# Attention rows transposed inside the last projection chunk, and another order on VectorE in the branch merge

## The chip, the cores and the metric

The kernel runs on one core of one Trainium2 chip. The metric is the device time of the whole program in microseconds (us), lower is better. Three timed runs of the kernel before lie between 2477.99 and 2490.73 us, with a median of 2486.15 us.

## What is computed

Two transformer blocks of two layers each, over 256 rows of 1024 channels, all in float32. The change touches only the mixer of the first block, which runs once per layer. Cut to that part, the reference is:

```python
for l in range(2):
    ...
    h = rms_norm(x, mix_norm[l])
    (nq, ..., ngate, sq, sk, sv, wq, wk, wv, bgate) = jnp.split(h @ w_in[l], SPLIT_POINTS, axis=-1)
    y_nsa = nsa_attention(...)             # 512 channels
    y_sb = stick_breaking_attention(...)   # 256 channels
    y_swa = swa_sink_attention(...)        # 256 channels
    g = jax.nn.sigmoid(bgate).reshape(B, S, 3, 1024)
    merged = (g[:, :, 0] * (y_nsa @ w_up_nsa[l]) + g[:, :, 1] * (y_sb @ w_up_sb[l])
              + g[:, :, 2] * (y_swa @ w_up_swa[l]))
    x = x + merged @ w_out[l]
    ...
```

## The kernel before

The 256 rows are two tiles (t = 0, 1) of 128 partitions. Weights come in chunks of at most 128 x 2048 numbers (1 MB), loaded by SyncE into a ring of four slots, one transfer per chunk, in program order. A slot is loaded again when TensorE has finished the chunk in it (`chunks_done`).

Every product with a weight is made from three products of rounded parts. ScalarE writes the rounded weight (RH, two buffers, line 1366), VectorE the rest, weight minus RH (RL, line 1792). Both steps are called `split`. The activations have the same two parts, HTH (ScalarE, line 1351) and HTL (VectorE, line 1776), made by `ht_copy` from a transposed copy that TensorE left in PSUM. In `split_products`, TensorE runs RH x HTH (line 646) and RH x HTL (line 647) for the first items, waits for RL, runs RL x HTH (line 650) for those items, and then the remaining items with all three products each. A chunk has 24 products of 512 columns, or 48 of 256 columns.

The mixer's projection `h @ w_in` has 23 chunks, numbered 0 to 22 (loop over `j` on TensorE, over `i` on the other engines, N1 = 23). A projection chunk does the 8 items of row tile 0 first (its RL products come behind them), then the 8 items of row tile 1. The results of even chunks are copied out by ScalarE (line 1517), those of odd ones by VectorE (line 2066). The three attention branches run in pieces between the chunks. Their rows collect in Y; the last piece, the compressed branch, is made by TensorE behind chunk 21 (line 984, `oc_ready`) and added into Y by VectorE in turn 22 (line 2051, `src_ready`).

Behind chunk 22 come, on every engine in this order:

- TensorE transposes Y (`transpose_y`, line 699, 16 transposes into PSUM banks 2 to 5), and ScalarE and VectorE copy the result into HTH and HTL. Chunk 22 reads these same two buffers, so nothing of this can stand inside it.
- Chunks 23 and 24 (`w_up_nsa`, banks 4 to 7), 25 (`w_up_sb`, banks 0 to 3) and 26 (`w_up_swa`, banks 4 to 7). Chunk 26 waits until VectorE has read chunk 24's result (`rows_taken`).
- Meanwhile ScalarE turns the gate columns of the projection into sigmoids (lines 1531 and 1533).
- VectorE merges the branches: TMP = bank 4..7 x gate 0 (line 2081), Y = bank 0..3 x gate 1 (line 2086), TMP += Y (line 2087), and then, per row tile, Y = bank 4..7 x gate 2 (line 2093) and Y += TMP (line 2094, `merged_rows`). Each instruction waits for the one before it (`link`).
- TensorE transposes the merged Y in two halves (lines 711 and 715), ScalarE and VectorE copy it into HTH and HTL, and chunks 27 to 30 (`w_out`) follow. Chunk 27 starts when the first of four pieces of HTL is there.

The splits stand by hand between these steps. On VectorE the split of chunk 27 stands ahead of line 2086.

Of the kernel before, what the change touches and what calls it, by code (L numbers as in the profile page):

```python
# [10 lines left out]
ALU = mybir.AluOpType  # L11
# [3 lines left out]
P = 128  # L15
S = 256
T = S // P
D = 1024
K = D // P
# [6 lines left out]
W1 = [256] * 9 + [24] + [256] * 13  # L26
N1 = len(W1)
# [160 lines left out]
def build(nc, a, out, con, hot_rev, hot, vect, scratch):  # L188
    ctx = ExitStack()
    with ctx:  # L190
# [3 lines left out]
        def over(name, shape, at, dtype=F32R):  # L194

            return nc.alloc_sbuf_tensor_at(name, shape, dtype, offset=at).ap()
# [16 lines left out]
        at_tt = nc.sbuf_base  # L213
# [45 lines left out]
        RINGS = over("RINGS", [P, ESLOTS, SLOT], at_ring, F32)  # L259
        RL = over("RL", [P, ESLOTS, SLOT], at_ring)  # L260
        RH3 = over("RH3", [P, SLOT], at_kd)
        GH, GL = (over(n, [P, 22, S], at_proj + 4 * i * 22 * S) for i, n in enumerate(("GH", "GL")))
        MEMH, MEML = (over(n, [P, K, S], at_proj + 4 * (T * D_IN2 + i * K * S)) for i, n in enumerate(("MEMH", "MEML")))
        EHH, EHL = (over(n, [P, 4, S], at_proj + 4 * (T * D_IN2 + 2 * K * S + i * 4 * S)) for i, n in enumerate(("EHH", "EHL")))
# [33 lines left out]
        def spread(ap, at, n):  # L298

            return bass.AP(tensor=ap.tensor, offset=ap.offset, ap=[*ap.ap[:at], [0, n], *ap.ap[at:]])  # L300
# [150 lines left out]
        def tr1(l, k):  # L451
            return l * 5 + k
# [9 lines left out]
        def rows_src(block, l):  # L462
            return l if block == 0 else L + l
# [159 lines left out]
        def _(pe):  # L623
# [7 lines left out]
                pe.wait_ge(ring_full[slot], ring.full())  # L631
                return RINGS[:, slot, :]

            def split_products(width, early, items, ht=None, half=None):

                slot = ring.next()
                splits.n += 1  # L640

                pe.wait_ge(wh_ready, splits.v + splits.n)
                listed = items(splits.buffer(RH, RH3)[:, 0:width], RL[:, slot, 0:width])

                def rounded(dst, a_, b_, start, stop, left):
                    mm(dst, a_[0], b_[0], start=start, stop=False)  # L646
                    mm(dst, a_[0], b_[1], start=False, stop=False) if left else mm(dst, a_[1], b_[0], start=False, stop=False)  # L647

                def rest(dst, a_, b_, start, stop, left):
                    return mm(dst, a_[1], b_[0], start=False, stop=stop) if left else mm(dst, a_[0], b_[1], start=False, stop=stop)  # L650

                for i, item in enumerate(listed[:early]):
                    if ht is not None and i < K and i % 2 == 0:
                        ht_wait(ht, i // 2)
                    rounded(*item)

                pe.wait_ge(wl_ready, splits.v + splits.n)
                for item in listed[:early]:
                    last = rest(*item)
                if half is not None:  # L660
                    last.then_inc(half, 1)
                for item in listed[early:]:
                    rounded(*item)
                    last = rest(*item)
                last.then_inc(chunks_done, 1)
# [6 lines left out]
                             (rhs[0][:, k, :], rhs[1][:, k, :]), k == 0, k == K - 1, True) for c in range(2) for k in range(K)]  # L672
                split_products(SLOT, K, items, ht)

            def to_rows(width, bank_of, lhs, at=0, ht=None):

                def items(wh, wl):
                    wh, wl = (w.rearrange("p (k n) -> p k n", n=width) for w in (wh, wl))
                    return [(PS[:, bank_of(t), at * t:at * t + width], (lhs[0][:, k, t * P:(t + 1) * P], lhs[1][:, k, t * P:(t + 1) * P]),
                             (wh[:, k, :], wl[:, k, :]), k == 0, k == K - 1, False) for t in range(T) for k in range(K)]  # L680
                split_products(K * width, K if at else 2 * K, items, ht)

            def add_rows(bank, lhs, k0, first, end, tiles=T, half=None):

# [37 lines left out]
            def transpose_y(n, made, bank=0):  # L722

                pe.wait_ge(ht_l, n * 4 + 4)
                pe.wait_ge(src_ready, made + 1)
                transpose_rows(Y, n, bank)

            def ht_wait(n, bank=3):

                pe.wait_ge(ht_l, n * 4 + bank + 5)  # L730
# [36 lines left out]
            def rows_product(lhs, nchunk, bank, k0=0, ht=None, half=None):  # L767

                for j in range(nchunk):
                    if ht is not None:  # L770
                        ht_wait(ht, k0 // 2 + j)
                    add_rows(bank, lhs, k0 + 2 * j, j == 0, j == nchunk - 1, half=half if j == nchunk - 1 else None)
# [5 lines left out]
            for l in range(L):  # L778
# [82 lines left out]
                for j in range(N1):  # L861
                    if j >= 2:
                        col_taken(j - 2)
                    to_rows(W1[j], lambda t: j % 2, HT, at=256, ht=n if j == 0 else None)
                    if 8 <= j < 8 + NU:
                        if j == 8:
                            pe.wait_ge(tt_a, l * 4 + 3)
# [117 lines left out]
                                          VCB.rearrange("p h d -> p (h d)"), start=True, stop=True)  # L985
                        last.then_inc(oc_ready, 1)

                n = tr1(l, 2)
                transpose_y(n, rows_src(0, l), 2)
                ht_wait(n)  # L990
                col_taken(21)
                col_taken(22)
                rows_product(HT, 2, 4)
                rows_product(HT, 1, 0, k0=4)

                pe.wait_ge(rows_taken, l + 1)
                rows_product(HT, 1, 4, k0=6, half=up_half)
                n = tr1(l, 3)
                transpose_halves(Y, n, merged_rows, 2 * l + 1)
                rows_product(HT, 4, 4, ht=n, half=rows_half)  # L1000
# [322 lines left out]
        def _(act):  # L1323
# [21 lines left out]
            def ht_copy(n, dst, gains=None, tiles=K, bank=0):  # L1345

                for b in range(4):

                    act.wait_ge(tr_ready, n * 4 + b + 1)
                    if gains is None or 2 * b >= tiles:  # L1350
                        A(dst[0][:, 2 * b:2 * b + 2, :], PS[:, bank + b, :].rearrange("p (k n) -> p k n", k=2), ACT.Copy).then_inc(ht_h, 1)
                    else:
                        A(dst[0][:, 2 * b, :], PS[:, bank + b, 0:S], ACT.Copy, scale=LV[:, gains + 2 * b:gains + 2 * b + 1])
                        A(dst[0][:, 2 * b + 1, :], PS[:, bank + b, S:2 * S], ACT.Copy, scale=LV[:, gains + 2 * b + 1:gains + 2 * b + 2]).then_inc(ht_h, 1)
# [61 lines left out]
            for l in range(L):  # L1416
# [32 lines left out]
                for i in range(N1):  # L1449
# [53 lines left out]
                    if i == 21:  # L1503
                        act.wait_ge(pct_ready, l + 1)
                        A(PTF[:, 0, 0:512], PS[:, 7, :], ACT.Copy).then_inc(pct_taken, 1)
                    if 9 <= i < 9 + NU:
                        exps(i - 9)
                    if i in (14, 15, 16):
# [16 lines left out]
                        ahead.skip(2)  # L1525
                        split(SLOT, 6)

                ht_copy(tr1(l, 2), HT, bank=2)
                act.wait_ge(col_d, cols_d + N1 // 2)
                act.wait_ge(col_a, cols_a + N1 // 2 + 1)  # L1530
                A(PROJ[:, :, BG:BG + D], PROJ[:, :, BG:BG + D], ACT.Sigmoid).then_inc(branch_gates, 1)
# [223 lines left out]
        def _(dve):  # L1755
# [11 lines left out]
                ring.next()  # L1767
                dve.wait_ge(chunks_done, ring.done())

            def ht_copy(n, dst, gains=None, tiles=K, bank=0):  # L1770

                for b in range(4):

                    dve.wait_ge(ht_h, n * 4 + b + 1)
                    if gains is None or 2 * b >= tiles:
                        TTn(dst[1][:, 2 * b:2 * b + 2, :], PS[:, bank + b, :].rearrange("p (k n) -> p k n", k=2), dst[0][:, 2 * b:2 * b + 2, :].bitcast(F32),  # L1776
                            ALU.subtract).then_inc(ht_l, 1)
                    else:
                        for k in (2 * b, 2 * b + 1):
                            last = V.scalar_tensor_tensor(dst[1][:, k, :], PS[:, bank + b, (k % 2) * S:(k % 2 + 1) * S], LV[:, gains + k:gains + k + 1],  # L1780
                                                          dst[0][:, k, :].bitcast(F32), ALU.mult, ALU.subtract)
                        last.then_inc(ht_l, 1)


            ahead, splits = Ring(), Splits()
# [78 lines left out]
            for l in range(L):  # L1864
# [83 lines left out]
                for i in range(N1):  # L1948
# [95 lines left out]
                        dve.wait_ge(osb_ready, l + 1)  # L2044
                        V.tensor_copy(Y[:, :, 512:768], PS[:, 6, :].rearrange("p (t n) -> p t n", t=2))
                    if i == 22:
                        dve.wait_ge(oc_ready, l + 1)
                        for t in range(T):
                            for r in range(2):
                                y = Y[:, t, 0:512].rearrange("p (g r x) -> p r g x", g=2, r=2)[:, r]  # L2050
                                last = TTn(y, y, PS[:, 4 + t, r * 256:(r + 1) * 256].rearrange("p (g x) -> p g x", g=2), ALU.add)
                        last.then_inc(src_ready, 1)
                    if 9 <= i < 9 + NU:
                        softmax(i - 9)
                    if 11 <= i < 11 + NU:
# [8 lines left out]
                    if i % 2:  # L2064
                        w = W1[i]
                        TTn(PROJ[:, :, OFF1[i]:OFF1[i] + w], PS[:, 1, :].rearrange("p (t n) -> p t n", t=2)[:, :, 0:w],
                            spread(SMALL[:, 4:6], 2, w), ALU.mult).then_inc(col_d, 1)
                    if i <= 10 or i >= 16:
                        split(K * W1[i + 2] if i + 2 < N1 else SLOT)
                    elif i in (12, 13):  # L2070
                        ahead.skip(2)
                        split()

                ht_copy(tr1(l, 2), HT, bank=2)
                split()
                ring.n += 1
                chunk()
# [3 lines left out]
                TTn(TMP, high, bg[0], ALU.mult).then_inc(rows_taken, 1)  # L2081
                split()
                chunk()
                split()
                dve.wait_ge(branch_gates, 2 * l + 2)
                link(TTn(Y, low, bg[1], ALU.mult))
                link(TTn(TMPF, TMPF, YF, ALU.add))
                for t in range(T):
# [3 lines left out]
                        chunk()  # L2092
                    link(TTn(Y[:, t, :], high[:, t, :], bg[2][:, t, :], ALU.mult))
                    TTn(Y[:, t, :], TMP[:, t, :], Y[:, t, :], ALU.add).then_inc(merged_rows, 1)
                ht_copy(tr1(l, 3), HT)
                split()
                for j in range(3):
                    split()
# [430 lines left out]
```

## Time and profile before

| | before |
|---|---|
| median of three timed runs | 2486.15 us |
| the profiled execution, its time | 2483.38 us |
| its span, first to last instruction | 2481.6 us |
| TensorE products busy | 2362.2 us, 95% of the span |
| VectorE busy | 1541.1 us, 62% |
| ScalarE busy | 1185.4 us, 48% |
| GpSimd busy | 71.7 us, 3% |
| mean granted clock of TensorE | 0.961 of 2.4 GHz |
| chain of work that ended last | TensorE 87%, VectorE 7%, ScalarE 3% |

The chain of work that ended last is the sequence of instructions, each released by the one before, that leads to the end of the program. Work outside it is hidden. The trace has a timeline (instructions of one engine in order of time, neighbours of one line merged), a view of waits, and a view that gives busy times and the granted clock of any stretch.

### The profile page before, as it was taken

Reading aid. Unit: us, or ns where it says so; the run is one execution under the profiler, and the core shown is the slowest. Engines: PE = TensorE matmul, PEld = TensorE weight load, DVE = VectorE, ACT = ScalarE, POOL = GpSimd, SP = SyncE. Lnnn points to the kernel's source line nnn. Section 1 sums busy time; section 2 is a strip of 40 time slices with the busy share of each in tenths; the row PEclk is TensorE's granted clock in tenths of the full one; section 3 lists DMA queues with packets and bytes.
Section 4 is the critical chain, followed back from the end, with each engine's and each line's share of the span. In section 5 each row is a group of like instructions: output and inputs, shape, how many; then the busy total and the mean of one; then the engine's idle time right before and its main releaser. Section 6 shows DMA issues by size and latency. Waiting matters only on the chain.

```text
span 2481.6 us, 34563 instructions
## 1 busy us (share of the span) xinstructions
PE 2362.2 (95%) x15120; PEld 2126.2 (86%) x15120; DVE 1541.1 (62%) x1421; ACT 1185.4 (48%) x1154; POOL 71.7 (3%) x84
## 2 busy tenths in 40 slices
PE   8999999799999998998999999799998999799998
PEld 8998889699899888887997999688887999688886
DVE  4655556566466446456664556478887556478887
ACT  3333543443343344434433445267775444267775
POOL 1000100000000001000000000000001000000000
PEclk9999899899999998999999999799999999799999
DMA  6554334355555543434555455389996455379995
GB/s 216 187 187 153 121 105 153 119 170 187 187 170 187 187 155 103 155 103 145 194 187 179 144 183 171 120 288 348 347 367 229 152 173 178 121 282 347 354 361 198
DMA packets 309612, 490.92 MB, mean 198 GB/s; under 512 B 15348, under 2 KB 204964, under 8 KB 309456
## 3 DMA queue, kind: packets, MB, share of 16 engines
q1 hardware_dynamic: 305696, 475.35, 56.3%
q0 software_dynamic: 2912, 10.13, 1.3%
q10 hardware_dynamic: 848, 3.15, 0.3%
q8 instruction: 123, 2.02, 0.3%
q14 instruction: 33, 0.27, 0.0%
HBM read 487.52 MB, written 1.07 MB: 197 GB/s over the span
## 4 chain that ended last, share of the span: by engine, by line
PE 87%; DVE 7%; ACT 3%; issue 1%; POOL 1%; DMA 0%; DVEq 0%; POOLq 0%; ACTq 0%
PE PS L646 26%; PE PS L647 26%; PE PS L650 25%; ACT RH L1366 2%; DVE RL L1792 2%; PE PS L1258 1%; PE PS L857 1%; PE PS L822 1%; PE PS L1191 1%; PE PS L1264 1%; PE PS L807 1%; DVE HTL L1776 1%; ACT PR L1432 0%; POOL SMALL L597 0%; DVE HTL L1780 0%
## 5 line engine op out<-in xcount | busy, mean ns | idle before, releaser
L1792 DVE TENSOR_TENSOR RL<-RINGS,RH 128x2048 fp32r<-128x2048 f32 x450 | 1018.3, 2265 | 638.0 <-ACT RH L1366 635.1
L1366 ACT ACTIVATE RH<-RINGS 128x2048 fp32r<-128x2048 f32 x450 | 852.0, 1894 | 834.4 <-PE PS L650 833.9
L646 PE MATMUL PS<-RH,HTH 128*128 128x256 f32 (+3 forms) x1888 | 627.9, 343 | 25.0 <-DVE HTL L1776 16.5
L647 PE MATMUL PS<-RH,HTL 128*128 128x256 f32 (+3 forms) x1888 | 614.1, 335 | 0.0
L650 PE MATMUL PS<-RL,HTH 128*128 128x256 f32 (+3 forms) x1888 | 450.5, 330 | 0.0
L646 PEld LDWEIGHTS PS<-RH,HTH 128*128 128x128 f32 x1888 | 373.7, 198 | 66.6 <-DVE HTL L1776 17.7
L646 PE MATMUL PS<-HTH,RH 128*128 128x256 f32 x1536 | 408.2, 284 | 9.2 <-ACT RH L1366 5.0
L647 PE MATMUL PS<-HTL,RH 128*128 128x256 f32 x1536 | 405.0, 282 | 0.0
L647 PEld LDWEIGHTS PS<-RH,HTL 128*128 128x128 f32 x1888 | 374.7, 198 | 32.6 <-issue 0.2
L650 PEld LDWEIGHTS PS<-RL,HTH 128*128 128x128 f32 x1888 | 332.4, 195 | 34.0
L650 PE MATMUL PS<-HTH,RL 128*128 128x256 f32 x1536 | 324.4, 283 | 0.0
L646 PEld LDWEIGHTS PS<-HTH,RH 128*128 128x128 f32 x1536 | 292.0, 190 | 12.9 <-issue 10.8
L647 PEld LDWEIGHTS PS<-HTL,RH 128*128 128x128 f32 x1536 | 291.6, 190 | 0.1
L650 PEld LDWEIGHTS PS<-HTH,RL 128*128 128x128 f32 x1536 | 244.6, 190 | 0.0
L646 PE MATMUL PS<-RH,GH 128*128 128x512 f32 x352 | 139.8, 397 | 0.0
L647 PE MATMUL PS<-RH,GL 128*128 128x512 f32 x352 | 137.9, 392 | 0.0
L647 PE MATMUL PS<-RH,EHL 128*128 128x512 f32 x256 | 100.7, 393 | 0.0
L646 PE MATMUL PS<-RH,EHH 128*128 128x512 f32 x256 | 100.5, 392 | 0.0
L650 PE MATMUL PS<-RL,GH 128*128 128x512 f32 x352 | 90.2, 391 | 0.0
L646 PEld LDWEIGHTS PS<-RH,GH 128*128 128x128 f32 x352 | 66.1, 188 | 16.2
L650 PEld LDWEIGHTS PS<-RL,GH 128*128 128x128 f32 x352 | 66.1, 188 | 14.9
L647 PEld LDWEIGHTS PS<-RH,GL 128*128 128x128 f32 x352 | 66.1, 188 | 14.4
(397 smaller groups left out, 2193.0 us busy)
## 6 DMA issues: line engine op xcount, KB each, us to landing
RINGS<-w_in SPq DMA_DIRECT2D x64, 1024.0 KB, 5.2
RINGS<-w_gate SPq DMA_DIRECT2D x64, 1024.0 KB, 5.7
RINGS<-w_up SPq DMA_DIRECT2D x64, 1024.0 KB, 5.6
RINGS<-w_down SPq DMA_DIRECT2D x64, 1024.0 KB, 5.4
RINGS<-ffn_w_gate SPq DMA_DIRECT2D x44, 1024.0 KB, 5.2
RINGS<-ffn_w_up SPq DMA_DIRECT2D x44, 1024.0 KB, 5.2
RINGS<-ffn_w_down SPq DMA_DIRECT2D x44, 1024.0 KB, 4.9
RINGS<-w_out SPq DMA_DIRECT2D x16, 1024.0 KB, 4.9
```

What stands on the lines that cost most here:

```text
L646: mm(dst, a_[0], b_[0], start=start, stop=False)
L647: mm(dst, a_[0], b_[1], start=False, stop=False) if left else mm(dst, a_[1], b_[0], start=False, stop=False)
L650: return mm(dst, a_[1], b_[0], start=False, stop=stop) if left else mm(dst, a_[0], b_[1], start=False, stop=stop)
L807: last = nc.tensor.transpose(PS[:, 4 + i // 4, (i % 4) * P:(i % 4 + 1) * P], PRF[:, u % 2, i * P:(i + 1) * P], IDENT)
L822: last = mm(PS[:, 6, s_ * HD:(s_ + 1) * HD], PTF[:, u % 2, i * P:(i + 1) * P], PROJ[:, b, vc:vc + HD], start=(b == 0), stop=(b == t))
L857: last = mm(PS[0:64, 7, kv * 256:(kv + 1) * 256], BT[:, kv, i * 8 + r, :], w[:, r, :], start=(i + r == 0), stop=(i == 1 and r == 7))
L1191: last = nc.tensor.transpose(PS[:, 2 + at // 512, at % 512:at % 512 + P], EHID[:, t, k * P:(k + 1) * P], IDENT)
L1258: last = mm(PS[:, 6 + i, k * P:(k + 1) * P], X[:, t, (4 * i + k) * P:(4 * i + k + 1) * P], SEAT[:, g, t, :], start=(t == 0), stop=(t == T ...
L1264: return mm(PS[:, 6 * t + h, :], SEATT[:, g, t, :], YSEAT[g][part][:, h, :], start=(g + part == 0), stop=(g + part == NG_))
L1366: A(splits.buffer(RH, RH3)[:, 0:width], RINGS[:, slot, 0:width], ACT.Copy).then_inc(wh_ready, 1)
L1776: TTn(dst[1][:, 2 * b:2 * b + 2, :], PS[:, bank + b, :].rearrange("p (k n) -> p k n", k=2), dst[0][:, 2 * b:2 * b + 2, :].bitcast(F32), AL ...
L1792: TTn(RL[:, slot, 0:width], RINGS[:, slot, 0:width], splits.buffer(RH, RH3)[:, 0:width].bitcast(F32), ALU.subtract).then_inc(wl_ready, 1)
```

## The change

Three edits, in each of the two layers:

1. Y is transposed in the middle of chunk 22, between its first eight items and the rest (`between`), and the copies go into YT, which lies over the first 16 of the 20 tiles of TT. Chunks 23 to 26 read YT.
2. For that, VectorE adds the compressed branch into Y in turn 21, ahead of the split of chunk 23. `ht_copy` moves into turn 22, on both engines ahead of the wait for chunk 22. TensorE's waits for the results of chunks 21 and 22 move behind chunks 23 and 24.
3. VectorE's split of chunk 27 moves from ahead of line 2086 to behind the first piece of the merged rows' HTL (`behind`).

```diff
+        YT = [over(n, [P, K, S], at_tt + 4 * i * K * S) for i, n in enumerate(("YTH", "YTL"))]
...
-            def split_products(width, early, items, ht=None, half=None):
+            def split_products(width, early, items, ht=None, half=None, between=None):
...
                 if half is not None:
                     last.then_inc(half, 1)
+                if between is not None:
+                    between()
                 for item in listed[early:]:
...
-                    to_rows(W1[j], lambda t: j % 2, HT, at=256, ht=n if j == 0 else None)
+                    to_rows(W1[j], lambda t: j % 2, HT, at=256, ht=n if j == 0 else None,
+                            between=(lambda: transpose_y(tr1(l, 2), rows_src(0, l), 2)) if j == N1 - 1 else None)
...
-                n = tr1(l, 2)
-                transpose_y(n, rows_src(0, l), 2)
-                ht_wait(n)
+                ht_wait(tr1(l, 2))
+                rows_product(YT, 2, 4)
                 col_taken(21)
                 col_taken(22)
-                rows_product(HT, 2, 4)
-                rows_product(HT, 1, 0, k0=4)
+                rows_product(YT, 1, 0, k0=4)
...
-                rows_product(HT, 1, 4, k0=6, half=up_half)
+                rows_product(YT, 1, 4, k0=6, half=up_half)
...
# ScalarE
+                    if i == 22:
+                        ht_copy(tr1(l, 2), YT, bank=2)
...
-                ht_copy(tr1(l, 2), HT, bank=2)
...
# VectorE
-            def ht_copy(n, dst, gains=None, tiles=K, bank=0):
+            def ht_copy(n, dst, gains=None, tiles=K, bank=0, behind=None):
...
+                    if b == 0 and behind is not None:
+                        behind()
...
                     if i == 22:
-                        dve.wait_ge(oc_ready, l + 1)
-                        for t in range(T):
-                            for r in range(2):
-                                y = ...
-                                last = TTn(y, y, ..., ALU.add)
-                        last.then_inc(src_ready, 1)
+                        ht_copy(tr1(l, 2), YT, bank=2)
...
+                    if i == 21:
+                        (the five removed lines, behind the result of chunk 21 is copied out)
...
-                ht_copy(tr1(l, 2), HT, bank=2)
                 split()
...
                 TTn(TMP, high, bg[0], ALU.mult).then_inc(rows_taken, 1)
                 split()
                 chunk()
-                split()
                 dve.wait_ge(branch_gates, 2 * l + 2)
...
-                ht_copy(tr1(l, 3), HT)
+                ht_copy(tr1(l, 3), HT, behind=split)
```

## Rows read from the trace of the kernel before

**Rows 1.** Page, first line.
```profile
span 2481.6 us, 34563 instructions
```
**Rows 2.** Waits of PE, 425 to 480 us: total us, times, longest.
```profile
PE PS L711 <- DVE Y L2094: 6.4, 1, 6.4
PE PS L646 <- DVE HTL L1776: 5.8, 1, 5.8
```
**Rows 3.** Timeline of PE, layer 0: start, us, instruction, [idle before, releaser].
```profile
426.65 1.89 PE L984 MATMUL PS<-VCB,PT 128*128 128x256 f32 x8
...
431.23 0.28 PE L646 MATMUL PS<-RH,HTH 128*128 128x256 f32 x1
...
434.12 1.91 PE L699 MATMUL PS<-CON,Y 128*128 128x128 f32 x16
441.80 0.80 PE L646 MATMUL PS<-RH,HTH 128*128 128x512 f32 x1 [5.77 <-DVE HTL L1776]
...
449.59 0.40 PE L646 MATMUL PS<-RH,HTH 128*128 128x512 f32 x1
...
455.15 0.40 PE L646 MATMUL PS<-RH,HTH 128*128 128x512 f32 x1
...
458.87 1.99 PE L650 MATMUL PS<-RL,HTH 128*128 128x512 f32 x8
...
472.74 1.94 PE L711 MATMUL PS<-CON,Y 128*128 128x128 f32 x8 [6.35 <-DVE Y L2094]
...
477.14 0.80 PE L646 MATMUL PS<-RH,HTH 128*128 128x512 f32 x1
```
**Rows 4.** Chain that ended last: start of chunk 28, layer 0.
```profile
484.57 0.23 PE PS L646
```
**Rows 5.** Timeline of DVE, layer 0.
```profile
431.09 1.40 DVE L2051 TENSOR_TENSOR Y<-Y,PS 128x256 f32<-128x256 f32 x4
...
463.25 2.29 DVE L1792 TENSOR_TENSOR RL<-RINGS,RH 128x2048 fp32r<-128x2048 f32 x1 [3.42 <-ACT RH L1366]
465.46 2.28 DVE L2086 TENSOR_TENSOR Y<-PS,PROJ 128x2048 f32<-128x2048 f32 x1
...
473.76 1.23 DVE L2094 TENSOR_TENSOR Y<-TMP,Y 128x1024 f32<-128x1024 f32 x1
476.40 2.48 DVE L1776 TENSOR_TENSOR HTL<-PS,HTH 128x512 fp32r<-128x512 f32 x4 [1.41 <-ACT HTH L1351]
```
**Rows 6.** Timeline of ACT, layer 0.
```profile
436.85 2.05 ACT L1351 ACTIVATE HTH<-PS 128x512 fp32r<-128x512 f32 x4
...
440.21 1.91 ACT L1531 ACTIVATE PROJ<-PROJ 128x2048 f32<-128x2048 f32 x1
...
451.68 3.61 ACT L1533 ACTIVATE PROJ<-PROJ 128x4096 f32<-128x4096 f32 x1
...
461.24 1.92 ACT L1366 ACTIVATE RH<-RINGS 128x2048 fp32r<-128x2048 f32 x1 [3.91 <-PE PS L650]
```
**Rows 7.** Page, part 6: ring transfers of w_out, us from issue to landing.
```profile
RINGS<-w_out SPq DMA_DIRECT2D x16, 1024.0 KB, 4.9
```
**Rows 8.** Timelines of PE, then DVE, layer 1.
```profile
1107.62 0.79 PE L646 MATMUL PS<-RH,HTH 128*128 128x512 f32 x1 [5.77 <-DVE HTL L1776]
...
1124.61 1.99 PE L650 MATMUL PS<-RL,HTH 128*128 128x512 f32 x8
...
1130.93 2.28 DVE L2086 TENSOR_TENSOR Y<-PS,PROJ 128x2048 f32<-128x2048 f32 x1
```
**Rows 9.** Stretches elsewhere: busy PE, PEld, DVE, ACT, POOL; then PEclk, DMA share, GB/s.
```profile
273.50:276.00 2.50, 0.04 (x1) 0.00 (x0) 1.94 (x3) 2.49 (x2) 0.53 (x1) 0.97 0.51 137
276.00:279.40 3.40, 3.36 (x17) 3.39 (x17) 1.29 (x3) 0.88 (x3) 0.00 (x0) 0.52 0.61 212
1476.30:1479.10 2.80, 0.04 (x1) 0.03 (x1) 1.11 (x2) 2.40 (x2) 0.00 (x0) 1.00 0.53 140
1479.10:1482.00 2.90, 2.90 (x13) 2.38 (x14) 1.58 (x1) 0.00 (x0) 0.00 (x0) 1.00 0.57 232
```

More of the change, by code:

```diff
@@ L673, in to_columns, with to_rows @@
                 split_products(SLOT, K, items, ht)
-            def to_rows(width, bank_of, lhs, at=0, ht=None):
+            def to_rows(width, bank_of, lhs, at=0, ht=None, between=None):
                 def items(wh, wl):
@@ L680, in items @@
                              (wh[:, k, :], wl[:, k, :]), k == 0, k == K - 1, False) for t in range(T) for k in range(K)]
-                split_products(K * width, K if at else 2 * K, items, ht)
+                split_products(K * width, K if at else 2 * K, items, ht, between=between)
             def add_rows(bank, lhs, k0, first, end, tiles=T, half=None):
@@ L2046, in _ @@
                     if i == 22:
-                        dve.wait_ge(oc_ready, l + 1)
-                        for t in range(T):
-                            for r in range(2):
-                                y = Y[:, t, 0:512].rearrange("p (g r x) -> p r g x", g=2, r=2)[:, r]
-                                last = TTn(y, y, PS[:, 4 + t, r * 256:(r + 1) * 256].rearrange("p (g x) -> p g x", g=2), ALU.add)
-                        last.then_inc(src_ready, 1)
+                        ht_copy(tr1(l, 2), YT, bank=2)
                     if 9 <= i < 9 + NU:
@@ L2067, in _ @@
                             spread(SMALL[:, 4:6], 2, w), ALU.mult).then_inc(col_d, 1)
+                    if i == 21:
+                        dve.wait_ge(oc_ready, l + 1)
+                        for t in range(T):
+                            for r in range(2):
+                                y = Y[:, t, 0:512].rearrange("p (g r x) -> p r g x", g=2, r=2)[:, r]
+                                last = TTn(y, y, PS[:, 4 + t, r * 256:(r + 1) * 256].rearrange("p (g x) -> p g x", g=2), ALU.add)
+                        last.then_inc(src_ready, 1)
                     if i <= 10 or i >= 16:
```

## The prediction

> **What bounds the kernel now.** I read the page's busy shares and its chain of work first: TensorE is busy 95% of the span and carries 87% of the chain, so time is won only where TensorE stands still or runs at the lower clock. The view of TensorE's waits then gives the places. The two that the change can touch come once per layer, 5.8 us for HTL and 6.4 us for the merged rows [rows 2]. The timeline shows what stands around them.
>
> First pause: the 16 transposes start at 434.12 and take 1.91 us, so they end at 436.03, and chunk 23 starts at 441.80 after 5.77 us of idling [rows 3]. In between ScalarE and VectorE finish chunk 24's split and make HTH and HTL. The first product behind the pause takes 0.80 us where those at the start of chunks 24 and 25 take 0.40 [rows 3]: the granted clock fell to 1.2 GHz while TensorE idled. Chunk 23 therefore lasts from 441.80 to 449.59, 7.79 us, against 5.56 us for chunk 24 (449.59 to 455.15) [rows 3].
>
> Second pause: chunk 25 ends at 458.87 + 1.99 = 460.86 [rows 3], but line 2086, the first that needs it, starts at 465.46 [rows 5]. Ahead of it in VectorE's queue stands the split of chunk 27, which waits for the RH that ScalarE writes from 461.24 [rows 6] and then takes 2.29 us [rows 5]. From the start of line 2086 to the end of the merge (473.76 + 1.23 = 474.99) there are 9.53 us of linked work [rows 5], and chunk 27 starts 2.15 us behind that, at 477.14 [rows 3].
>
> **The change part by part.** Sums are made against the profiled execution, span 2481.6 us [rows 1], time 2483.4 us; its time is 2.8 us under the median of the runs and inside their scatter.
>
> *Transposes in chunk 22, results in memory of their own.* Nothing is added: 16 transposes, 4 copies on ScalarE and 4 subtractions on VectorE move ahead. TensorE keeps their 1.8 us or so. The question is whether anything arrives too late in the new place.
> - The transposes need Y complete. The compressed branch's products end at 426.65 + 1.89 = 428.54 [rows 3]. VectorE has copied out chunk 21 by then, adds from 428.6 for 1.40 us [rows 5] and is done at 430.0. TensorE reaches the middle of chunk 22 at 431.23 [rows 3]. Slack 1.2 us. Queued behind the new wait on VectorE is the split of chunk 23, which moves from about 431.1 to 432.3 at its end; chunk 23 wants it at about 440.
> - Transposes from 431.25 to 433.05, then the second half of chunk 22 until about 436.2 (chunk 22 ends at about 434.3 now, while the transposes behind it are starting; 1.8 for the transposes and 0.1 from the bound below come on top). ScalarE copies as the pieces come, 2.05 us [rows 6], done about 434.1; VectorE, free at 432.3, is done about 435.0 (2.48 us for four [rows 5]). Slack 1.2 us before chunk 23 wants them at 436.2.
> - ScalarE passes its copies ahead of the copying out of chunk 22 and the split of chunk 24. That split now ends at about 438.8 instead of 436.95, chunk 24 wants it at 441.8. The sigmoid of gate 0 still ends near 442.1, as before (440.21 + 1.91 [rows 6]), since what was ahead of it is only reordered. The RH of chunk 25 then comes at 444.0, the second sigmoid (3.61 us [rows 6]) at 447.6, the RH of chunk 26 at 449.5.
> - VectorE: TMP from 447.5 to 449.8, RL of chunk 26 until 452.1. Chunk 26 starts at 452.9 and needs both, RL not before 454.7.
> - No DMA is issued or moved by the edit itself, and neither SyncE nor GpSimd has a step inside it. SyncE's loads follow `chunks_done` and so come earlier with it: the first w_out chunk is released at the end of chunk 23, 441.8, lands 4.9 us later [rows 7], and ScalarE wants it at 452.9.
>
> So the pause of 5.77 us goes, and with it the fall of the clock: 7.79 - 5.56 = 2.23 us. Together 8.0 us. What the trace of before does not show is 16 transposes in the middle of a chunk. Lower bound 0 (they cost the same in any place); upper bound 0.4 us, by which the first product behind the transposes and the pause is longer than one in full flow (0.80 against 0.40 [rows 3]). Most of those 0.4 is the clock, so I take 0.1. Per layer 7.9 us.
>
> *The split of chunk 27 behind the first piece.* Line 2086 can start about 0.2 us behind chunk 25's end instead of 465.46 - 460.86 = 4.6 us: gain 4.4 us in layer 0. Layer 1: 1130.93 - (1124.61 + 1.99) = 4.33 [rows 8], gain 4.1. What is late next is the linked merge of 9.5 us itself, which starts at 453.1 and ends at 462.5; TensorE ends chunk 26 at 458.45 and idles for some 1.6 us before the first half of the rows, where it idled 6.35 us. The moved split costs 2.29 us behind the first subtraction. Chunk 27 starts at 464.6 and wants that RL after its 16 first products, at 468.3 or later; it is there at 467.0. The three other HTL pieces end at about 469, the next is wanted at 470.2 at the earliest. Both covers hold, the thinner by 1.3 us; without them each late us costs one.
>
> *The clock in the second pause.* Before, it cost 484.57 - 477.14 = 7.43 us [rows 3, 4] instead of 5.56 for chunk 27, and some 0.3 us in the last transposes. After, TensorE idles 1.6 us, transposes, waits about 1.5 us, transposes, waits 1 us: 6.1 us with only 1.8 to 2 us of work. Nearest rows: a pause of 2.5 us was followed by 1.2 GHz [rows 9], one of 2.8 us was not [rows 9]. Broken up over 6 us it is nearer to the first, so I take the clock as fallen again: gain 0, bounds 0 and 1.87 + 0.3 = 2.2 us per layer.
>
> Sum: layer 0, 7.9 + 4.4 = 12.3; layer 1, the same pause of 5.77 us and the same slow first product (0.79 us) [rows 8], 7.9 + 4.1 = 12.0. Together 24.3 us. From 2483.4 that is 2459.1 us, from the median 2461.8. I say 2460.
>
> **The rivals.**
> 1. *The clock stays up in the second pause.* Another 2 x 2.2 = 4.4 us: 2454.7 to 2457.4 us, say 2456. For it: the single pauses are shorter than 2.8 us [rows 9]. Against it: there are three in a row. The Trainium skill ("TensorE: Matmul & The Clock Gate", Part 1 on the HAM clock gate) says that an idle array is throttled and that what follows starts at the lower rate; by that rule the clock falls here and the sum stays 2460, without it 2456. The trace agrees at the pause of 2.5 us and does not at that of 2.8 us.
> 2. *A thin cover breaks.* If VectorE's copies for YT come 2 us later than I lay out, or RL of chunk 27 comes behind the sixteenth product, TensorE waits there. Losing the whole merge gain gives back 8.5 us: 2468.5 us. For it: slacks of only 1.2 to 1.3 us at three places. Against it: all durations there are rows of the same instructions.
> 3. *The change doesn't do what it says.* TensorE still stands still behind chunk 22, because YT or the operands of chunk 23 come only after it (copying out of chunk 22 first, say). Then only the merge gain is left, 8.5 us: 2477 us, within 0.5%. The order of the queues speaks against it, since `ht_copy` stands ahead of the wait for chunk 22 on both engines.
> 4. *Slower.* The transposes put 16 short products of 128 columns into a dense stream, and the clock could fall there and stay down. Place: from 431 us on, chunks 23 and later. Price: at half the clock a chunk takes up to twice its 5.56 us, so 5.6 us more. It decides from four chunks per layer on: 2 x 4 x 5.56 = 44.5 us against 24.3 gained, 2503.6 us; with three it would be 33.4 against 24.3, or 2492.5, still within 0.5% of no change. Against it: the 16 transposes take 1.91 us right behind chunk 22 now, and the 8 at the second pause 1.94 [rows 3], so the former run at full clock.
>
> **How the numbers follow.** Forecast 2460 us with 0.55; rival 1 0.27; rival 2 0.11; rival 3 0.04; rival 4 0.03. The range goes from 2449 (rival 1, less the 6 to 8 us by which single runs of before lie off their median) to 2471 (rival 2 with a little of the same). 0.5%, 12.4 us, is about what a measurement of this kernel can tell from no change. Faster by more than that: the forecast, rivals 1 and 2 except for a small part: 0.92. Within it: rival 3 and what is left: 0.05. Slower: 0.03.
>
> **What would show it.** In the profile after: the transposes of line 699 of both layers inside chunk 22, two groups of 256-column products around them; no idle time ahead of the first 512-column product and none of that kind over 0.45 us in chunk 23; line 2086 within 0.3 us of chunk 25's end; chunk 27 starting some 28.4 us behind chunk 22's end (now 477.14 - 434.3 = 42.8); chunk 27 lasting 7.4 us (forecast) or 5.6 us (rival 1). The prediction is wrong if TensorE waits for `src_ready` in chunk 22, for HTL at chunk 23, or for RL of chunk 27, or if the clock falls at a place where it was full before.

## The result

| | before | after |
|---|---|---|
| median of four timed runs each | 2486.28 us | 2454.22 us |
| ratio, 95% interval | | 0.988, 0.9845 to 0.9916 |
| the profiled execution, its time | 2483.38 us | 2456.64 us |
| its span | 2481.6 us | 2454.8 us |
| mean granted clock of TensorE | 0.961 | 0.967 |

The change makes the kernel 1.2% faster, 32.1 us between these two medians. The forecast was 2460 us with a range of 2449 to 2471; the median lies inside it, but the case that came was the first rival, the clock that stays up, at "2454.7 to 2457.4". Taken over all runs of both kernels in this study, the changed one has a mean of 2455.8 us (14 runs, standard deviation 3.9) and the one before 2484.7 us (23 runs, 3.4): 28.9 us, with a standard error of about 1.3.

### The profile page after: what moved, and what is told of

It is laid out like the page before. It is cut to its first block, busy times and chain, and to the rows that moved or that the text cites. A ratio compares the mean times of both kernels' runs of the same rounds, so it can differ in the third digit from the quotient of the medians.

```text
span 2454.8 us, 34563 instructions
## 1 busy us (share of the span) xinstructions
PE 2352.6 (96%) x15120; PEld 2119.5 (86%) x15120; DVE 1541.3 (63%) x1421; ACT 1185.7 (48%) x1154; POOL 71.7 (3%) x84
## 4 chain that ended last, share of the span: by engine, by line
PE 88%; DVE 6%; ACT 3%; issue 1%; POOL 1%; DMA 0%; POOLq 0%; DVEq 0%; ACTq 0%
PE PS L647 26%; PE PS L648 26%; PE PS L651 26%; ACT RH L1368 1%; PE PS L1260 1%; DVE RL L1797 1%; PE PS L860 1%; PE PS L825 1%; PE PS L1193 1%; PE PS L1266 1%; PE PS L810 1%; ACT PR L1434 0%; DVE HTL L1783 0%; POOL SMALL L598 0%; POOL SMALL L584 0%
## 5 line engine op out<-in xcount | busy, mean ns | idle before, releaser
L647 PE MATMUL PS<-RH,HTH 128*128 128x256 f32 (+3 forms) x1824 | 599.2, 339 | 15.1 <-DVE HTL L1779 6.8
L648 PE MATMUL PS<-RH,HTL 128*128 128x256 f32 (+3 forms) x1824 | 586.4, 332 | 0.0
L651 PE MATMUL PS<-RL,HTH 128*128 128x256 f32 (+3 forms) x1824 | 433.3, 328 | 0.0
L647 PEld LDWEIGHTS PS<-RH,HTH 128*128 128x128 f32 x1824 | 360.3, 198 | 51.8 <-issue 13.3
L648 PEld LDWEIGHTS PS<-RH,HTL 128*128 128x128 f32 x1824 | 361.3, 198 | 29.4 <-issue 0.2
L651 PEld LDWEIGHTS PS<-RL,HTH 128*128 128x128 f32 x1824 | 320.3, 196 | 31.4
```

## The profile after

The page of the changed kernel: the span, and what TensorE is busy.

```profile
span 2454.8 us, 34563 instructions
...
PE 2352.6 (96%) x15120; PEld 2119.5 (86%) x15120; DVE 1541.3 (63%) x1421; ACT 1185.7 (48%) x1154; POOL 71.7 (3%) x84
```

The instructions are as many as before, and VectorE and ScalarE are busy as long as before. TensorE is busy 9.6 us less with the same 15120 products. In the two stretches that the change touches it is 11.4 us less (90.25 us before, 78.81 after), in products that ran at 1.2 GHz before; elsewhere it is 1.8 us more. (In the changed kernel the lines 646, 647, 650 are 647, 648, 651; 699 is 702; 711 and 715 are 714 and 718; 2086 and 2094 are 2091 and 2099.)

TensorE's waits between 426 and 480 us, total us, times, longest. They answer to [rows 2], where the two largest were 6.4 and 5.8:

```profile
PE PS L714 <- DVE Y L2099: 1.8, 1, 1.8
PE PS L718 <- DVE Y L2099: 1.2, 1, 1.2
PE PS L647 <- DVE HTL L1779: 0.8, 1, 0.8
```

The 5.8 us ahead of chunk 23 are gone. The timeline of TensorE, layer 0, answers to [rows 3]: start, us, instruction, idle before.

```profile
431.54 1.91 PE L702 MATMUL PS<-CON,Y 128*128 128x128 f32 x16
433.20 0.36 PE L647 MATMUL PS<-RH,HTH 128*128 128x256 f32 x1
...
436.14 0.39 PE L647 MATMUL PS<-RH,YTH 128*128 128x512 f32 x1
...
460.29 1.06 PE L714 MATMUL PS<-CON,Y 128*128 128x128 f32 x8 [1.76 <-DVE Y L2099]
462.59 1.09 PE L718 MATMUL PS<-CON,Y 128*128 128x128 f32 x8 [1.24 <-DVE Y L2099]
464.44 0.50 PE L647 MATMUL PS<-RH,HTH 128*128 128x512 f32 x1 [0.76 <-DVE HTL L1779]
...
470.12 0.39 PE L647 MATMUL PS<-RH,HTH 128*128 128x512 f32 x1
```

The transposes stand inside chunk 22 with no wait ahead of them, and chunk 23 (the first product of 512 columns) follows chunk 22 without a gap and at full clock, 0.39 us instead of 0.80. Behind chunk 26 one long pause of 6.35 us (and a short one of 0.36 between the halves) has become three of 1.76, 1.24 and 0.76 us. Each half of the transposes takes 1.06 and 1.09 us; before, the first took 1.94 [rows 3]. VectorE in the same time, which answers to [rows 5]:

```profile
428.88 1.41 DVE L2073 TENSOR_TENSOR Y<-Y,PS 128x256 f32<-128x256 f32 x4 [1.03 <-PE PS L988]
430.21 2.28 DVE L1797 TENSOR_TENSOR RL<-RINGS,RH 128x2048 fp32r<-128x2048 f32 x1
432.80 2.48 DVE L1779 TENSOR_TENSOR YTL<-PS,YTH 128x512 fp32r<-128x512 f32 x4 [0.31 <-ACT YTH L1353]
...
453.01 2.29 DVE L2091 TENSOR_TENSOR Y<-PS,PROJ 128x2048 f32<-128x2048 f32 x1 [1.06 <-PE PS L651]
...
463.70 0.69 DVE L1779 TENSOR_TENSOR HTL<-PS,HTH 128x512 fp32r<-128x512 f32 x1 [1.16 <-ACT HTH L1353]
464.31 2.28 DVE L1797 TENSOR_TENSOR RL<-RINGS,RH 128x2048 fp32r<-128x2048 f32 x1
466.50 1.88 DVE L1779 TENSOR_TENSOR HTL<-PS,HTH 128x512 fp32r<-128x512 f32 x3
```

The sum into Y ends at 430.3, 1.2 us before TensorE wants it. YTL is whole at 435.3, 0.9 us before chunk 23. The merge (line 2091) waits for TensorE now and no longer for a split. RL of chunk 27 is there at 466.6; its RL products start at 468.27.

The granted clock behind chunk 26 (busy PE, PEld, DVE, ACT, POOL; then PEclk, DMA share, GB/s):

```profile
458.50:460.30 1.80, 0.04 (x2) 0.04 (x1) 1.77 (x3) 1.68 (x1) 0.00 (x0) 1.00 0.34 50
460.30:464.40 4.10, 2.15 (x16) 1.67 (x16) 2.91 (x4) 1.57 (x4) 0.00 (x0) 1.00 0.59 240
464.40:470.10 5.70, 5.66 (x24) 4.62 (x25) 5.70 (x5) 0.73 (x2) 0.00 (x0) 1.00 0.00 0
```

It is 1.00 throughout, although TensorE idles for almost 4 of the 6 us up to chunk 27.

**Where the time went.** In every trace I measured one stretch on TensorE's timeline: from the start of the compressed branch's products behind chunk 21 to the start of chunk 28. In us:

| | layer 0 | layer 1 | gain, both |
|---|---|---|---|
| before | 57.75 | 57.45 | |
| after, three profiles | 43.14 to 43.17 | 43.16 to 43.18 | 28.9 |

The stretch of before ends where the first product of chunk 28 starts, which is a line that neither the rows nor the prediction show:

```profile
484.40 0.40 PE L646 MATMUL PS<-RH,HTH 128*128 128x512 f32 x1
```

So the stretches alone are enough for the difference of the means; that the two agree to 0.1 us is luck, given the standard error. In layer 0 the 14.6 us are: 5.97 up to chunk 23, 2.20 from there to the end of chunk 26, 4.84 from there to chunk 27, 1.58 in chunk 27. In layer 1 they are 5.95, 2.12, 4.56 and 1.66.

Single runs of one kernel differ by several us, and the traces show part of the reason. The clock also falls at some fifteen other places, and which of them differs from run to run. Added up in steps of 1 us over the whole span, the time at the lower clock is 194.7 us in the profile of before and 160.5, 150.8 and 170.8 us in the three of the changed kernel, whose spans are 2454.8, 2449.2 and 2457.7 us. It is not the whole reason: of the timed runs of the changed kernel two have the same mean granted clock, 0.968, and last 2454.3 and 2460.9 us.

## The experiments

All of them are judged by the stretch, which repeats within 0.04 us as long as the clock does the same, and by the whole time where several rounds were run.

**The changed kernel beside the others (e0_after, e10_after).** No edit.

> The changed kernel again, on the chip of the three beside it, so that they are compared with it and not only with the kernel before. If the gain is what the two traces show for the two stretches (14.6 and 14.3 us), 28.9 us under the kernel before. If part of the gain lay elsewhere or was scatter, 25 us or less.

> The changed kernel once more, five rounds, beside the kernel with w_up_nsa last. 31 us under the kernel before, as in the rounds before.

Medians 2454.28 us (four runs, ratio 0.9878, 0.9862 to 0.9895) and 2457.35 us (six runs, 0.9891, 0.9872 to 0.991), 31.6 and 27.7 us under the kernel before on the same chip, where 28.9 and 31 were expected. Both are within the scatter. In both profiles, in both layers, the clock stays at full speed through the stretch.

**The transposes alone (e1_transposes).**

```diff
                 split()
                 chunk()
+                split()
                 dve.wait_ge(branch_gates, 2 * l + 2)
...
-                ht_copy(tr1(l, 3), HT, behind=split)
+                ht_copy(tr1(l, 3), HT)
```

> The change without its third edit: transposes inside chunk 22, but VectorE's split of chunk 27 stays ahead of the merge. Theory (the first pause and its low clock are worth 7.9 us per layer, and the second stays as it was, 6.4 us of idling and a fallen clock behind it): 15.8 us under the kernel before, chunk 27 lasting 7.4 us in both layers. Rival (the low clock at the second pause came from the first one, so the transposes alone keep it up): chunk 27 lasts 5.6 us, 19.6 us under the kernel before or more.

Median 2473.44 us, ratio 0.9956 (0.9939 to 0.9973). The stretches are 48.66 and 48.47 us, 18.1 us under before together. The medians differ by only 12.4 us, and the interval ends at 15.2: the whole time shows less than the stretches of the one profile do. That profile, 2466.01 us, is the fastest of the four runs, and the others have the same mean granted clock (0.961 to 0.963 against 0.962), so the clock isn't what makes them longer. Where the rest went stays open. The second pause and what follows, layer 0:

```profile
467.55 1.94 PE L714 MATMUL PS<-CON,Y 128*128 128x128 f32 x8 [6.32 <-DVE Y L2100]
469.85 1.97 PE L718 MATMUL PS<-CON,Y 128*128 128x128 f32 x8 [0.36 <-DVE Y L2100]
```
```profile
471.90:478.30 6.40, 6.35 (x24) 5.16 (x25) 3.98 (x4) 0.74 (x2) 0.00 (x0) 0.87 0.00 0
```

The pause and the slow transposes are as before, as the theory had it, so the low clock there comes from that pause and not from the first one: the rival falls. But chunk 27 lasts 6.4 us and not 7.4; the clock came back earlier in it (0.87 over the chunk). That, about 0.9 us per layer, is most of why the gain in the stretch is 18.1 and not 15.8.

**The moved split alone (e2_split).** The third edit put into the kernel before.

```diff
... (`ht_copy` gets `behind` as in the change)
                 chunk()
-                split()
                 dve.wait_ge(branch_gates, 2 * l + 2)
...
-                ht_copy(tr1(l, 3), HT)
+                ht_copy(tr1(l, 3), HT, behind=split)
```

> The kernel before with the third edit alone: the split of chunk 27 behind the first piece of HTL. Theory (the length of one uninterrupted pause decides on the clock, and this edit shortens the second one from 6.35 us to below 2): merge gain 4.3 us plus 2.1 us of clock per layer, 12.8 us under the kernel before, chunk 27 lasting 5.6 us; e1 and e2 add up to the whole change. Rival (the clock stays up there only since nothing fell at the first pause): chunk 27 lasts 7.4 us, 8.6 us under the kernel before.

Median 2471.81 us, ratio 0.9951 (0.9934 to 0.9968); stretches 52.08 and 52.11 us, 11.0 us under before. Transposes, then chunk 27, layer 0:

```profile
470.10:474.50 4.40, 3.03 (x16) 2.40 (x16) 2.95 (x4) 1.58 (x4) 0.00 (x0) 0.75 0.57 231
474.50:480.60 6.10, 6.09 (x24) 4.99 (x25) 6.10 (x5) 0.69 (x2) 0.00 (x0) 0.90 0.00 0
```

Neither case came. The pauses are those of the changed kernel (1.79 and 1.24 us), yet the clock fell between the two halves of the transposes, in both layers, and rose again early in chunk 27, which lasts 6.2 us. In the stretches the parts add up: 18.1 + 11.0 = 29.1 us against 28.9 for both. That is partly chance: each part alone still has a fall behind chunk 26 that the whole has not, and each of these falls costs less than the one of before. The medians, 12.4 and 14.1 us under before, add up to 26.5 us against 31.6 for the whole on the same chip, within their intervals.

**A longer pause (e3_pause_long, e4_pause_mid).** The first step of the merge done twice, for both row tiles or for one.

```diff
+                link(TTn(Y, low, bg[1], ALU.mult))
                 link(TTn(Y, low, bg[1], ALU.mult))
```

> The changed kernel with the first step of the merge (line 2091, 2.3 us) done twice, so that TensorE's first pause behind chunk 26 grows from 1.8 to 4.1 us. Theory (one uninterrupted pause decides on the clock): the clock falls, the stretch up to chunk 28 grows by 2.3 + 2.0 us in each layer. Rival (the clock stays up because the transposes break the stretch, however long its parts): 2.3 us per layer and chunk 27 at 5.6 us.

> The same with only row tile 0 of that step done twice (1.2 us), first pause 3.0 us. The traces so far have a pause of 2.5 us with a fall and one of 2.8 us without, so the theory leaves it open here and the rival says no fall: 1.3 us per layer without a fall, 3.3 us with one.

e3: first pause 4.09 us. Layer 0 transposes, layer 1 pause and transposes:

```profile
465.60:470.00 4.40, 3.91 (x16) 3.11 (x16) 2.96 (x4) 1.37 (x3) 0.00 (x0) 0.50 0.06 23
...
1117.50:1121.60 4.10, 0.04 (x1) 0.00 (x0) 4.03 (x4) 1.91 (x1) 0.00 (x0) 1.00 0.70 244
1121.60:1126.00 4.40, 3.03 (x16) 2.42 (x16) 2.95 (x4) 1.34 (x3) 0.00 (x0) 0.64 0.03 11
```

The stretch grows by 4.5 and 4.2 us, 2.3 of it work and 2.1 and 1.9 the clock: the theory's numbers. But the fall comes inside the pause in layer 0 and behind it in layer 1. e4: first pause 3.02 us, the clock full during it and at 0.77 over the transposes, chunk 27 at 6.24 us; the stretch grows by 2.07 us in both layers, 1.3 of it work and 0.8 the clock. So there is a third case beside the two that I had priced, a short fall that costs 0.8 us.

**The covers (e5_add_late, e6_col_waits).** e5 puts VectorE's sum into Y behind the split of chunk 23, as before the change; e6 puts TensorE's waits for chunks 21 and 22 back ahead of chunk 23.

```diff
# e6
+                col_taken(21)
+                col_taken(22)
                 rows_product(YT, 2, 4)
-                col_taken(21)
-                col_taken(22)
```

> The changed kernel with VectorE's sum for the compressed branch behind the split of chunk 23 in turn 21, where it stood in time before. It then ends at about 432.8 instead of 430.2, and TensorE reaches the middle of chunk 22 at 431.5. Theory (slack 1.2 us, each us beyond it costs one): TensorE waits 1.1 to 1.4 us inside chunk 22 in each layer, 2.5 us in all. Rival (the wait is taken up by idle time elsewhere): no change.

> The changed kernel with TensorE's waits for the results of chunks 21 and 22 ahead of chunk 23, where they stood before. ScalarE copies chunk 22 out until about 0.9 us behind its end. Theory: TensorE waits 0.9 to 1.1 us ahead of chunk 23 in each layer, 2 us in all, and the clock stays. Rival: nothing, since the weight loads of chunk 23 run ahead anyway.

e5, then e6, TensorE's timeline:

```profile
431.85 1.94 PE L702 MATMUL PS<-CON,Y 128*128 128x128 f32 x16 [1.25 <-DVE Y L2078]
```
```profile
440.21 0.47 PE L647 MATMUL PS<-RH,YTH 128*128 128x512 f32 x1 [1.13 <-ACT PROJ L1521]
...
466.75 1.97 PE L718 MATMUL PS<-CON,Y 128*128 128x128 f32 x8 [1.24 <-DVE Y L2099]
```

The waits are there and of the size expected, 1.25 and 1.13 us; chunk 23 comes 1.45 and 1.29 us later. The stretch, however, grows by 3.0 and 3.7 us in e5 and by 2.2 us in both layers in e6. Behind chunk 26 both have the first two pauses of the changed kernel, 1.76 and 1.24 us, and the clock falls all the same: in e6 at the start of the second half of the transposes, in e5 in chunk 27 in layer 0 (7.23 us) and in the wait between the two halves in layer 1 (chunk 27 then takes 7.65 us). The expectation of e6, that the clock stays, was wrong. This was the surprise, and the next experiment is about it.

**The same stretch, later (e8_shift).** Nothing of the stretch's waits is touched; TensorE's products behind chunk 21 are issued twice.

```diff
-                        for t in range(T):
-                            for r in range(2):
+                        for t, r in [(t, r) for _ in range(2) for t in range(T) for r in range(2)]:
```

> The changed kernel with TensorE's products of the compressed branch behind chunk 21 done twice (the same values), so that everything behind them comes 1.6 us later and the pauses behind chunk 26 keep their lengths (1.8, 1.2 and 0.8 us). Theory (whether the clock falls there hangs on where the stretch lies in time, not on its pauses alone): with this shift the clock can fall as in the two kernels shifted by 1.3 and 1.4 us, behind the first transposes or in chunk 27, and the stretch grows by 1.6 plus 0.8 to 2.2 us. Rival (in those two it was the wait of TensorE inside or ahead of chunk 23 that brought the fall): the clock stays up and the stretch grows by 1.6 us alone.

The halves of the transposes on TensorE's timeline, layer 0, and the granted clock around them:

```profile
464.53 1.06 PE L714 MATMUL PS<-CON,Y 128*128 128x128 f32 x8 [1.77 <-DVE Y L2098]
466.84 1.97 PE L718 MATMUL PS<-CON,Y 128*128 128x128 f32 x8 [1.24 <-DVE Y L2098]
```
```profile
464.50:466.80 2.30, 1.06 (x8) 0.85 (x8) 2.25 (x2) 0.27 (x1) 0.00 (x0) 0.88 0.93 379
466.80:468.90 2.10, 1.97 (x8) 1.57 (x8) 0.71 (x2) 1.34 (x3) 0.00 (x0) 0.50 0.14 55
```

Chunk 23 comes 1.74 us later with no wait ahead of it, the pauses behind chunk 26 are 1.77 and 1.24 us as in the changed kernel, and the clock falls in the wait ahead of the second half of the transposes in both layers. The stretch is 47.0 us: 1.7 us of work and 2.1 us of clock over the changed kernel. So no wait of TensorE is needed for such a fall, and the rival falls. It is one profile of one kernel; what supports it is the place of the pauses.

That place can be read from the traces. Within each of the fourteen, the moments at which the granted clock changes lie on one even grid, within 4 ns, through the whole program. Take the place of the first pause behind chunk 26 as the time since the last grid moment:

| kernels with pauses of 1.8 and 1.2 us | the first pause begins behind a grid moment by | clock |
|---|---|---|
| changed kernel, three profiles | 1.4, 1.4; 1.7, 1.7; 1.4, 1.4 us (layers 0, 1) | stays full |
| e2, e6, e8 | 2.9, 2.9; 2.9, 2.9; 3.3, 3.4 us | falls |
| e5 | 0.2, 3.1 us | falls in chunk 27; falls between the halves |

All six stretches of the changed kernel lie together on this grid, and all eight that lost the clock with the same pauses lie elsewhere on it.

**The up projections in another order (e7_nsa_last, e11_nsa_last, e9_nsa_shift).** A version meant to beat the changed kernel: with the two chunks of w_up_nsa last, the sums of the other two branches run under them. Its core:

```diff
# TensorE
-                rows_product(YT, 2, 4)
+                rows_product(YT, 1, 4, k0=4)
                 col_taken(21)
                 col_taken(22)
-                rows_product(YT, 1, 0, k0=4)
+                rows_product(YT, 1, 0, k0=6)
...
-                rows_product(YT, 1, 4, k0=6, half=up_half)
+                rows_product(YT, 2, 4, half=up_half)
# VectorE
-                split()
-                ring.n += 1
                 chunk()
                 dve.wait_ge(branch_gates, 2 * l + 1)
-                TTn(TMP, high, bg[0], ALU.mult).then_inc(rows_taken, 1)
+                TTn(TMP, high, bg[1], ALU.mult).then_inc(rows_taken, 1)
                 split()
                 chunk()
                 dve.wait_ge(branch_gates, 2 * l + 2)
-                link(TTn(Y, low, bg[1], ALU.mult))
+                link(TTn(Y, low, bg[2], ALU.mult))
+                split()
                 link(TTn(TMPF, TMPF, YF, ALU.add))
+                ring.n += 1
```

e9 is this kernel with e8's edit. ScalarE makes the sigmoid of gate 1 first.

> A possible better version: the changed kernel with the order of the up projections turned, w_up_sb (banks 4 to 7), w_up_swa (banks 0 to 3), then the two chunks of w_up_nsa. What is left of the merge behind chunk 26 is one product and one sum per row tile, the rest runs under chunks 24 and 25. Theory (the linked merge is what TensorE waits for in the changed kernel, 9.5 us from the end of chunk 25): merged rows at about 2.6 us behind chunk 26 instead of 4.2, so 1.6 us per layer, 3 us under the changed kernel. Rival (something else comes late there, such as VectorE's splits or the sigmoids, which now have to be there for gate 1 first): no gain, or a wait ahead of chunk 25 of w_up_nsa.

> The kernel with w_up_nsa last, with the same products done twice. Its pauses behind chunk 26 are 1.6 and 0.8 us, with no pause ahead of the first transposes. Theory (shorter pauses keep the clock wherever they lie): chunk 27 at 5.7 us, the stretch 1.6 us longer than in that kernel without the shift. Rival (place in time decides here too): a fall behind the transposes, 0.8 us or more on top.

> The kernel with w_up_nsa last, five rounds. Theory (its stretches are 1.5 us shorter per layer, and what made it slower in four runs were falls of the clock elsewhere that come and go): 3 us under the changed kernel, 0 to 5 with the scatter. Rival (the falls elsewhere belong to this kernel): 2 to 4 us over it, as in the four runs.

TensorE in e7, layer 0, behind chunk 26:

```profile
460.85 1.06 PE L714 MATMUL PS<-CON,Y 128*128 128x128 f32 x8
463.47 1.09 PE L718 MATMUL PS<-CON,Y 128*128 128x128 f32 x8 [1.56 <-DVE Y L2100]
```

The first half of the transposes follows chunk 26 without a pause, and the stretch is 41.66 and 41.68 us, 1.5 us per layer under the changed kernel, as worked out. No wait comes ahead of chunk 25. With the shift (e9) the clock stays full and the stretch is 43.36 and 43.40 us, the 1.7 us of the added work alone. In the second profile of the version without a shift (e11) it is 41.67 us in layer 0, but 43.16 us in layer 1, where chunk 27 met a fall:

```profile
466.10:471.80 5.70, 5.66 (x24) 4.63 (x25) 5.70 (x5) 0.73 (x2) 0.00 (x0) 1.00 0.00 0
1112.00:1116.30 4.30, 1.98 (x17) 1.51 (x15) 3.11 (x4) 3.26 (x4) 0.00 (x0) 0.98 0.70 244
1116.30:1123.40 7.10, 7.10 (x24) 5.69 (x25) 6.09 (x5) 0.64 (x2) 0.00 (x0) 0.77 0.01 2
```

So the theory "shorter pauses keep the clock wherever they lie" is wrong too. The whole time does not show the 3 us: 2458.48 us (four runs, ratio 0.9885, 0.9858 to 0.9913) and 2459.26 us (six runs, 0.9897, 0.9879 to 0.9914), 4.2 and 1.9 us over the changed kernel beside it, with intervals that overlap. The time at the lower clock is larger in its profiles (178.4 us in e7, 171.2 in e11, the fall in its stretch included) than in e0_after (150.8), and about that of e10_after (170.8). e11 was to tell the two cases of its expectation apart, and by the medians the rival came, but 1.9 us is inside the scatter. Whether that belongs to this order or to the runs stays open; the version is not shown to be better.

## Why the prediction was right, and which step was not

- **What bounds the kernel, and where.** Right. Both places were read from the waits and the timeline of TensorE, and they are enough for the whole gain: 28.9 us in the stretches, 28.9 us between the means. That 2454.22 us lies inside the range is owed to the rival that was counted into it, not to the sum that gave 2460.
- **The first pause, 5.77 us less 0.1.** 5.97 us came. The transposes in the middle of the chunk cost next to nothing: the first product behind them lasts 0.36 us instead of 0.28, and the time up to chunk 23 grew by 1.71 us for them, where they took 1.91 at their old place. So the term was not a loss of 0.1 us but a gain of 0.2.
- **Its low clock, 2.23 us.** 2.20 us between chunk 23 and the end of chunk 26, 2.12 in layer 1. e1, with the transposes alone, has both terms in full.
- **The merge, 4.4 and 4.1 us.** The pause behind chunk 26 shrank by 4.59 us in layer 0 (6.35 to 1.76) and by 4.32 in layer 1 (6.08 to 1.76). Line 2091 starts at 453.01, 0.03 us behind the end of chunk 25, where I had allowed 0.2, and the linked work is 9.5 us as laid out.
- **The covers.** The sum into Y has the 1.2 us of slack that I worked out; e5 shows that beyond it each us is paid (1.25 us of wait). YTL has 0.9 us instead of 1.2, RL of chunk 27 1.7 us instead of 1.3. e6 shows what the moved waits were worth, 1.3 us per layer; I had listed them with edit 2 and given them no price of their own.
- **The clock in the second pause: wrong.** "I take the clock as fallen again: gain 0" is the step that failed. It stayed up in both layers of all three profiles of the changed kernel and gave 1.58 and 1.66 us in chunk 27 and 0.25 and 0.24 us in the transposes ahead of it, 3.7 us together; I had priced rival 1 at 4.4. Part of that price was a misread row: [rows 4] is a piece of the chain, and the first product of chunk 28 starts at 484.40 and not at 484.57, so chunk 27 took 7.26 us before and not 7.43. The stretches gave 28.9 us where the sum had 24.3; of the 4.6 us between them 3.7 are this step, and 0.9 are the terms above. The comparison that I chose it by, length of pause against fall, does not hold: with the same pauses the clock fell in e2, e5, e6 and e8. The Trainium skill ("TensorE: Matmul & The Clock Gate", Part 1 on the HAM clock gate) makes the lower rate the state behind an idle window, and calls that window free-running. I had used the rule as if any idle time were enough. The kernel before and e3, whose pauses of 6.35 and 4.09 us were followed by the lower clock, agree with the first half. e8 against the changed kernel, and the even grid on which the clock changes, agree with the second.
- **The price of a fall.** I had two values, 0 and 2.2 us. The runs show a short one of 0.8 us in e4 and e6 (chunk 27 at 6.2 us, clock about 0.9), one of 1.5 us in e11 and in layer 0 of e5, and 1.9 to 2.2 us in e3, in e8 and in layer 1 of e5.
- **The range.** Its lower end took single runs of before as 6 to 8 us off their median. They lie 4.6 above and 8.2 below it; the forecast doesn't change by that.

What stays open: what brings the stretch to its place. The three profiles of the changed kernel start the stretch at 426.96, 428.64 and 429.89 us of the span, but on the grid of the clock changes they start it 0.6, 0.9 and 0.6 us behind a moment (layer 1: 0.6, 0.8 and 0.6). e8 starts it at 0.8 in both layers and has 1.7 us more inside. So time since the start of the program is not what counts here. In ten of the fourteen traces both layers start the stretch 0.5 to 0.9 us behind a grid moment, so two layers are not two independent samples; why they do, no run tested. Which clock the timed runs without a profile had in the stretch isn't recorded.

## What to carry to other kernels

A step that needs only the previous step's data and a free buffer can be put into the middle of the last dense block ahead of it, so that the copies behind it run under the rest of the block: here 16 transposes cost 1.9 us behind the block and 1.7 us inside it, and the place was worth 8.1 to 8.2 us per layer. In a chain of linked steps that an engine waits for, look for work in the same queue that is wanted later than the chain: one split of 2.3 us and its wait for ScalarE were worth over 4 us per layer. Count what such a change gives in the stretch itself first, then bound the clock on top from both sides, and compare means of many runs where the gain of a version is about 3 us: single runs of one kernel were up to 13 us apart here.

## What the runs showed of the hardware

- The granted clock fell or stayed with the same pauses of 1.8, 1.2 and 0.8 us, depending on a shift of the whole stretch by 1.7 us (e8 against the changed kernel). No pause of e2, e6 or e8 in question was longer than 1.8 us.
- Within one trace all changes of the granted clock lie on one even grid, within 4 ns (all fourteen traces). The pauses that kept the clock began 1.4 to 1.7 us behind a moment of it (six stretches), those of the same lengths that lost it at 0.2 or at 2.9 us and more (eight stretches).
- A pause of 4.1 us in e3 ended at full clock in layer 1, and the clock fell behind it, while the transposes ran.
- A fall costs 0.8 us (e4, e6) to 2.2 us (e5, layer 1) in chunk 27 and the transposes ahead of it, by when the clock comes back.
- The run-to-run scatter of this one-core kernel, 3.4 to 3.9 us, goes in part with the time that TensorE spends at 1.2 GHz outside the stretches changed here: 150.8 us of it in a profile of 2449.2 us, 170.8 us in one of 2457.7 us of the same kernel. In the kernel before, runs of 2477.8 and 2478.0 us have a mean granted clock of 0.964 and runs of 2487.3 and 2489.9 us one of 0.959; in the changed one, runs of 2454.3 and 2460.9 us both have 0.968.
